# First forget gates computed from x before its norm, and the second half's recurrent steps placed at other slots

## The reference

```python
def rms_norm(x, g):
    y = x * rsqrt(mean(x * x, axis=-1) + RMS_EPS)
    return y * g

def trunk_layer(x, ...):
    h = rms_norm(x, g_mix_pre)
    proj = h @ w_in                      # q, f, i, g of the recurrence, q, k, v of attention
    f = lb + (1 - lb) * sigmoid(z_f)     # forget gate
    k = (1 - lb) * sigmoid(-z_f)
    o, state = gated_linear_recurrence(q, k, v, log(f), s0, chunk)
    rec = rms_norm(o, g_rec_out) * silu(z_g)          # the norm over each head
    mixed = concat([rec, attn]) @ w_out
    x = x + rms_norm(mixed, g_mix_post)
    h = rms_norm(x, g_mlp_pre)
    u = square(relu(h @ w_up))
    return x + rms_norm(u @ w_down, g_mlp_post)
```

## Time and profile before

| | us |
|---|---|
| median of 3 timed runs | 1590.98 (1590.57 to 1594.33) |
| the profiled execution, whole | 1592.15 |
| its span, first to last instruction | 1590.4 |
| mean granted TensorE clock, share of full | 0.993 |
| PE busy | 1536.7 |
| DVE busy | 997.5 |
| ACT busy | 850.3 |

### The profile page before, as it was taken

One profiled execution on the slowest core, in us unless ns is written; L12 is line 12 of the kernel. 1 busy time (PEld: TensorE's weight loads), 2 busy tenths in 40 slices (PEclk: granted clock), 3 DMA queues, 4 the chain that ended last, 5 costly groups with the idle time before them and its releaser, 6 DMA issues.

```text
span 1590.4 us, 29827 instructions
## 1 busy us (share of the span) xinstructions
PE 1536.7 (97%) x11984; PEld 1463.5 (92%) x11984; DVE 997.5 (63%) x1675; ACT 850.3 (53%) x1540; POOL 129.9 (8%) x165
## 2 busy tenths in 40 slices
PE   5999999899999999999999999998999999999996
PEld 5998789898999999999999987898899999999996
DVE  6683778774548655345887656878645675553466
ACT  6445655476455755234664565445755465551552
POOL 4120123000000000000002100330000000000000
PEclk9999999999999999999999999999999999999998
DMA  6644664353454555334443467343534545552453
GB/s 202 202 137 164 235 217 133 107 179 107 134 165 153 167 190 180 114 107 150 155 146 120 141 219 266 121 141 115 169 104 148 164 154 179 182 183 80 133 154 118
DMA packets 83237, 247.89 MB, mean 156 GB/s; under 512 B 8691, under 2 KB 26483, under 8 KB 82972
## 3 DMA queue, kind: packets, MB, share of 16 engines
q1 hardware_dynamic: 83100, 245.98, 48.2%
HBM read 234.13 MB, written 14.44 MB: 156 GB/s over the span
## 4 chain that ended last, share of the span: by engine, by line
PE 86%; DVE 8%; ACT 2%; issue 2%; DMA 1%; SPq 0%; DVEq 0%; ACTq 0%
PE ps L1030 68%; PE ps L1027 7%; PE ps L1083 3%; DVE w_rest L1347 2%; PE ps L1233 1%; PE ps L1220 1%; PE ps L1248 1%; DVE reg L1385 1%; DMA kc<-kcT 1%; DVE x L1389 1%; DVE norm_every L1370 1%; DVE square_sum L1360 1%; ACT w_high L749 1%; PE ps L1058 1%; PE ps L1206 0%
## 5 line engine op out<-in xcount | busy, mean ns | idle before, releaser
L1030 PE MATMUL ps<-h_high,w_rest 128*128 128x320 f32 (+1 forms) x1920 | 581.2, 303 | 8.5 <-DVE h_rest L1409 5.8
L1030 PE MATMUL ps<-h_rest,w_high 128*128 128x320 f32 (+1 forms) x1920 | 570.5, 297 | 0.0
L1030 PE MATMUL ps<-h_high,w_high 128*128 128x320 f32 (+1 forms) x1920 | 570.2, 297 | 0.0
L749 ACT ACTIVATE w_high<-w_raw 128x1024 fp32r<-128x1024 f32 x384 | 402.1, 1051 | 231.4 <-PE ps L1030 231.4
L1347 DVE TENSOR_TENSOR w_rest<-w_raw,w_high 128x1024 fp32r<-128x1024 f32 x380 | 473.0, 1250 | 74.7 <-ACT w_high L749 74.6
L1030 PEld LDWEIGHTS ps<-h_high,w_rest 128*128 128x128 f32 x1920 | 366.4, 191 | 26.1 <-issue 21.6
L1030 PEld LDWEIGHTS ps<-h_rest,w_high 128*128 128x128 f32 x1920 | 366.6, 191 | 0.8 <-issue 0.4
L1030 PEld LDWEIGHTS ps<-h_high,w_high 128*128 128x128 f32 x1920 | 366.5, 191 | 0.0
L1030 PE MATMUL ps<-u_high,w_rest 128*128 128x320 f32 (+1 forms) x1024 | 306.0, 299 | 2.8 <-DVE u_rest L1451 2.4
L1030 PE MATMUL ps<-u_high,w_high 128*128 128x320 f32 (+1 forms) x1024 | 303.8, 297 | 0.0
L1030 PE MATMUL ps<-u_rest,w_high 128*128 128x320 f32 (+1 forms) x1024 | 303.7, 297 | 0.0
(11 more groups left out here) (181 smaller groups left out, 1600.0 us busy)
## 6 DMA issues: line engine op xcount, KB each, us to landing
w_raw<-w SPq DMA_DIRECT2D x384, 512.0 KB, 3.6
kc<-kcT SPq DMA_DIRECT2D x16, 512.0 KB, 8.7
vc<-vc SPq DMA_DIRECT2D x16, 512.0 KB, 7.1
s_in<-s SPq DMA_DIRECT2D x8, 512.0 KB, 5.9
ss<-s_in SPq DMA_DIRECT2D x8, 512.0 KB, 5.9
bias<-rel_scratch SPq DMA_DIRECT2D x8, 512.0 KB, 4.5
rel_scratch<-rel_row SPq DMA_DIRECT2D x1, 2560.0 KB, 12.3
bias<-rel_scratch SPq DMA_DIRECT2D x8, 256.0 KB, 5.4
```

Of the source, the lines that this page charges most:

```text
L749: A.activation(whi[:, v % RING], raw[:, v % RING], ACT.Copy).then_inc(S["w_hi"], 1)
L1030: last = pe.matmul(ps[:, bank, 0:n], wt[:, slot, c, :], xt[:, c, :], **flags)
```

## The change

Two things, in one diff.

First products. ACT rounds `x * gain` (not yet normed) to `first_high`, DVE makes `first_rest`, and F0 to F3 of layer 0, half 0, multiply these. F0 and F1 are followed on PE by the norm's sum. Their results are multiplied by the inverse norm on DVE (`f_scaled`, into `tmp`) before ACT takes the two sigmoids from there. The six first products have six PSUM banks (`FIRST_BANKS`) instead of two. The first weight block is loaded ahead of x, the parameters behind x's first part, and DVE makes the remainder of block 0. ACT now rounds blocks 2 and 3 ahead of the norm's root, and blocks 4 and 5 (`N_SOON`) between the chunks of `pre`; DVE makes the remainders of blocks 4 and 5 within `pre` as well, ahead of the gates' arithmetic.

Second half's steps, in both layers: `upd` goes from behind IB 18 to behind IB 25, `out` from IB 23 to IB 27, `r_sum` from IB 25 to D0A 0, `r_spr` from IB 27 and U0A 0 to D0A 1 and D0A 2.

```diff
+FIRST_BANKS = (0, 1, 3, 4, 2, 7)
+N_FIRST = 4
+N_SOON = 2
...
-    put("IB", 18, "upd", 1)
+    put("IB", 25, "upd", 1)
...
-    put("IB", 23, "out", 1)
+    put("IB", 27, "out", 1)
...
-    put("IB", 25, "r_sum", 1)
-    put("IB", 27, "r_spr", 1, 0)
-    put("U0A", 0, "r_spr", 1, 1)
+    put("D0A", 0, "r_sum", 1)
+    put("D0A", 1, "r_spr", 1, 0)
+    put("D0A", 2, "r_spr", 1, 1)
...
         if o.i == 1:
+            here.insert(0, ("first_sum", 0))
             here.append(("rel", 0))
...
+            load(0)
             for c in range(0, KC, 2):
                 sp.dma_start(x[:, c:c + 2, 0:WIDE[0]], xT[:, c:c + 2, 0:WIDE[0]]).then_inc(S[f"x_part{c // 2}"], 16)
-            sp.dma_start(prm[:], par).then_inc(S["p_in"], 16)
-            for v in range(RING):
+                if c == 0:
+                    sp.dma_start(prm[:], par).then_inc(S["p_in"], 16)
+            for v in range(1, RING):
                 load(v)
...
                 if o.kind == "F":
+                    if o.n < N_FIRST:
+                        act.wait_ge(S["f_mul"], o.n + 1)
+                        src = tmp[:, o.n, 0:n]
                     A.activation(kb[o.h][:, o.k, :], src, ACT.Sigmoid, scale=-1.0)
...
             act.wait_ge(S["one_set"], 2)
+            act.wait_ge(S["p_in"], 16)
+            x_high(0)
+            high(0)
+            for p in range(1, 4):
+                x_high(p)
+            high(1)
             for p in range(4):
                 x_sq(0, 0, p)
-            high(0)
-            norm_sum(0, 0, 0)
-            high(1)
-            for p in range(4):
-                pre(0, 0, 0, p)
             high(2)
             high(3)
+            norm_sum(0, 0, 0)
             act.wait_ge(S["lb_set"], 2)
             A.activation(lb[:], lb[:], ACT.Exp).then_inc(S["lb_exp"], 1)
+            for p in range(4):
+                if p < N_SOON:
+                    act.wait_ge(S["blk"], p + 1)
+                    high(RING + p)
+                pre(0, 0, 0, p)
...
+            def f_scaled(o):
+                dve.wait_ge(S["blk"], o.n + 1)
+                V.tensor_tensor(tmp[:, o.n, 0:WIDE[0]], ps[:, bank_of(o), 0:WIDE[0]], every[:, 0:WIDE[0]], ALU.mult)\
+                    .then_inc(S["f_mul"], 1)
...
+            def x_low(c):
+                dve.wait_ge(S["x_hi"], c + 1)
+                V.scalar_tensor_tensor(first_l[:, c, :], x[:, c, 0:WIDE[0]], prm[:, 0, c:c + 1], first_h[:, c, :].bitcast(F32),
+                                       ALU.mult, ALU.subtract).then_inc(S["x_lo"], 1)
+
+            x_low(0)
+            x_low(1)
+            dve.wait_ge(S["w_hi"], 1)
+            V.tensor_tensor(wlo[:, 0], raw[:, 0], whi[:, 0].bitcast(F32), ALU.subtract).then_inc(S["w_lo_0"], 1)
+            for c in range(2, KC):
+                x_low(c)
             for p in range(4):
                 x_sq(0, 0, p)
-            norm_sum(0, 0, 0)
-            for p in range(5):
-                pre(0, 0, 0, p)
...
+            norm_sum(0, 0, 0)
+            dve.wait_ge(S["n_inv"], 1)
+            for o in outs[:2]:
+                f_scaled(o)
+            for p in range(5):
+                pre(0, 0, 0, p)
+                if p in (1, 4):
+                    rest(RING + p // 4)
```

More of the change, by code:

```diff
@@ L424, in build @@
             [place(f"bias1_{s}", [P, 2, 512], offset=o) for s, o in enumerate((o_vt[0], o_f))]]
+    first_h = place("first_high", [P, KC, WIDE[0]], F32R, offset=part(0, 8))
+    first_l = place("first_rest", [P, KC, WIDE[0]], F32R, offset=part(1, 0))
+    first_x = place("first_x", [P, KC, WIDE[0]], offset=part(1, 10))
     rel_sb = place("rel_sb", [P, NREL], offset=o_key[1])
@@ L448, in build @@
     free_at = {}
-    lo_of = {v: ("w_lo_p", v + 1) for v in range(RING)}
+    lo_of = {v: ("w_lo_p", v) if v else ("w_lo_0", 1) for v in range(RING)}
     for o in outs:
@@ L731, in a_spr @@
                                 ALU.subtract).then_inc(S["a_lo"], 1)
-            rest(0)
+            for v in range(1, RING):
+                rest(v)
             for c in range(1, KC, 2):
                 pool.wait_ge(S["h_hi"], c + 1)
-                V.tensor_tensor(hl[0][:, c, :], acc[0][:, c, :], hh[0][:, c, :].bitcast(F32), ALU.subtract).then_inc(S["h_odd"], 1)
-            for v in range(1, RING):
-                rest(v)
+                V.tensor_tensor(hl[0][:, c, :], first_x[:, c, :], hh[0][:, c, :].bitcast(F32), ALU.subtract).then_inc(S["h_odd"], 1)
             table = {"lev": lev, "wide": wide, "s_upd": s_upd, "kc_own": kc_own, "r_spr": r_spr, "a_spr": a_spr}
@@ L759, in x_sq @@
             def x_sq(l, h, p):
-                if h == 0:
-                    act.wait_ge(S[f"x_part{p}"], 16)
-                elif p == 0:
+                if h and p == 0:
                     act.wait_ge(S["x_in1"], 16)
@@ L1329, in a_spr, with first_sum @@
                     held[5 + i] = (S["a_scaled"], 8 * l + 4 * h + 2 * g + i + 1)
-            pe.wait_ge(S["one_set"], 2)
-            norm_sum(0, 0, 0)
-            table = {"norm_sum": norm_sum, "rel": rel, "lev": lev, "k_t": k_t, "v_t": v_t, "upd": upd, "out": out,
+            def first_sum(l):
+                pe.wait_ge(S["one_set"], 2)
+                norm_sum(0, 0, 0)
+            table = {"first_sum": first_sum, "norm_sum": norm_sum, "rel": rel, "lev": lev, "k_t": k_t, "v_t": v_t, "upd": upd, "out": out,
                      "s_rd": s_rd, "s_o": s_o, "s_upd": s_upd, "r_sum": r_sum, "r_spr": r_spr, "sc": sc_, "pt": pt_, "pv": pv,
@@ L1395, in pre @@
                 cols = slice(FIRST[h], FIRST[h] + n)
+                to = acc[h] if m else first_x
                 if p == 0:
                     dve.wait_ge(S["n_inv"], m + 1)
-                    if m == 0:
-                        dve.wait_ge(S["p_in"], 16)
                 if p < 4:
                     for c in (2 * p, 2 * p + 1):
-                        V.scalar_tensor_tensor(acc[h][:, c, :], x[:, c, cols], gain[:, c:c + 1], every[:, 0:n],
+                        V.scalar_tensor_tensor(to[:, c, :], x[:, c, cols], gain[:, c:c + 1], every[:, 0:n],
                                                ALU.mult, ALU.mult).then_inc(S["nap"], 1)
@@ L1416, in evict @@
                 n = WIDE[o.h]
[L1417 removed]
+                src = ps[:, bank_of(o), 0:n]
                 if o.kind in ("Q", "G"):
@@ L1730, in _ @@
                     rest(v)
-                late = [v + RING for v in free_at[o.n] if v + RING < n_loads]
+                late = [v + RING for v in free_at[o.n] if N_SOON <= v < n_loads - RING]
                 after(o)
```

39 lines of the change are left out of this document (27 added, 12 removed).

## The result

The changed kernel took **1598.43 us** (median of 5 runs, 1597.14 to 1600.17), the kernel before, timed beside it, 1591.7 (5 runs, 1590.57 to 1594.33). The ratio is 1.0039, 95% interval 1.0028 to 1.0049, so slower, by 4.5 to 7.8 us. The forecast was 1598.0. The profiled execution took 1600.17, with a span of 1598.4, 8.0 more than before.

What follows compares the result with a forecast made beforehand. PE, busy 97% of the span, was taken as the bound, so only its waits count. First products 4.3 plus second half's steps 2.8 gave 7.1 us slower, 1598.0 for the median; range 1587 to 1602, slower at chance 0.51.

Steps and rivals of the forecast that it cites:

- the sum of 7.1: Whole kernel: 4.3 us slower from the first products plus 2.8 slower from the second half's steps.
- Start of F0: First products: F0 starts at 11.2, 6.3 us earlier than before, with parameters taken to land at 6.8.
- Rival (d): Start: parameters still land at 8.2, F0 starts hardly earlier, time 1600; inside the forecast, given no separate chance.
- The root's end S: First products: the norm's root ends at 24.1 against 12.8 before; without POOL's hold about 22.8.
- From S to block 6: DVE and ACT work behind the root: block 6's remainder, which Q2 needs, ends at S+22.7 = 46.8.
- PE's wait and the clock: Ahead of Q2: PE waits 6.5 us from 40.3, half clock costs 2.0; behind Q3 PE is 4.3 later.
- The lower bound: First products: without holds S = 22.3, chain 2.0 shorter, block 6 at 43.0, hidden; at best 1.4 us faster.
- the upper bound: First products: parameters late (S = 25.5) and clock loss 2.4, 6.1 us slower; range stated up to +6.5.
- The second half's steps: Per layer: IB 22 sum 1.6 earlier, PE's wait 4.5, net 0.2 slower, new `pt` wait 1.25; 2.8 us for both layers.
- (a): First products: DVE catches up better, holds and handovers cost half, block 6 at 44 to 45; 1594, chance 0.24.
- (b): Behind IB 22: `upd` on DVE held the sum, PE's wait shrinks 1.6 per layer; 1592, chance 0.11.
- (c): At Q2: block 6's remainder ends by 40.3, PE keeps its 4.2 us lead; 1586.8 or 1585, chance 0.14.

Runs made afterwards that it cites:

- p1_nohold: `p1_only` with block 1's remainder made by DVE instead of POOL: 1594.01 us against 1592.3 for the kernel before, ratio 1.0007.
- p1_soon4: `p1_only` with `N_SOON = 4`, so blocks 6 and 7 are rounded and remaindered early too: 1596.18 us against 1592.83 for the kernel before.
- p1_defer: `p1_soon4` with F2 and F3 scaled ahead of the remainders, F0 to F3 arithmetic and second-half squares deferred: 1587.93 us against 1592.3 for the kernel before.
- p2_norm: The kernel before with only `r_sum` and `r_spr` moved to D0A 0, 1 and 2: 1594.48 us against 1592.3 for the kernel before.
- p2_only: The kernel before with only the second half's steps moved as in the change: 1593.66 us against 1592.83, ratio 1.0010.
- p2_fill: The kernel before with the second half's `upd` moved behind IB 22, ahead of the norm's sum: 1586.95 us against 1592.3, ratio 0.9965.
- p1_only: The changed kernel with the second half's steps back at their old slots: 1595.72 us against 1592.83 for the kernel before, ratio 1.0020.
- after_fill: The changed kernel with `upd` behind IB 22 and `out` back at IB 23: 1590.96 us against 1592.44 for the kernel before, ratio 0.9991.
- best: The kernel before with `p1_defer`'s first products, block 1's remainder on DVE and `upd` behind IB 22: 1580.45 us against 1592.44, ratio 0.9928.

## Why the prediction was right

**The time.** 1598.43 against 1598.0; the sum of 7.1 stands against 8.0 in the traces and 6.2 by the ratio (0.0039 times 1592), 4.5 to 7.8 by its interval. That the time agrees within 0.4 us is partly luck. The terms miss in both directions: the sum had 2.0 for the lower clock, where PE is 4.3 longer busy, and 5.1 of idle time, where 3.7 were added. The mechanism is what the rows below bear out.

**Start of F0.** 10.27, forecast 11.2. The parameters were there at 5.70 instead of the 6.8 that I took between 5.5 and 8.2. Rival (d), parameters late, is out.

**The root's end S.** 22.65, forecast 24.1. 1.1 of the difference is the parameters. That POOL's remainder holds the adds was right, and `p1_nohold` shows it: 1.07 us of S, where I had put 1.3 by the difference of the two estimates (24.1 and 22.8).

**From S to block 6.** Forecast S + 22.7; the remainder ends at 44.16 + 1.22, S + 22.7. It is right at its marks too: block 5's remainder ends at S + 13.2 (forecast 12.8), the scaling of F2 at S + 18.0, as forecast. What makes it long is what stands in the queue, which `p1_soon4` and `p1_defer` separate: the block alone sooner only moves the wait, with the arithmetic behind it the wait is gone. That is the shown cause of the first part's loss.

**PE's wait and the clock.** The wait is 4.6, forecast 6.5, as S came 1.45 sooner and Q1 ended about 0.5 later. The forecast had Q0 end 6.0 behind F3, for a product of 3.5, so it left room for waits there, and there are two for `h_rest`, 1.9 together. What it left out are the 3.4 us at half clock behind them, about 1.5 lost; F0's earlier start, 0.9, paid part of it. Behind the wait the loss was mis-sized the other way: from Q2 at 45.42, two products of 7.04 in all would give 52.46, and G0 came at 55.17, so 2.7 lost for the 2.0 I had charged. Together G0 is 3.67 late, forecast 4.3. The lower bound, block 6 at 43.0 and "hidden", was read wrongly: PE stands from 40.3, so 2.7 us of wait and the clock behind it belonged into it; and the upper bound comes to 6.1 by its terms, not 6.5.

**The second half's steps.** All three statements hold. The sum behind IB 22 moved 1.7 forward (forecast 1.6), PE's wait stayed (4.34, forecast 4.5), and the new wait at `pt` is 1.15 to 1.2 in each layer (forecast 1.25). Net 0.94 in layer 1, where the half-clock stretch is as long as before, and 2.09 in layer 0, where it is 6.8 us instead of 3.4: 3.0 in the sum, forecast 2.8. The size per layer was off in both directions, in layer 0 by the clock, for which the forecast had no term here; that the sum fits is luck in part. `p2_norm` shows that the norm's place alone brings the wait at `pt`, and its time alone (1.0012) is no less than that of `p2_only` (1.0010), so the rest of the part is too small for these runs to see.

**Rivals.** (a), DVE catching up by half, is out at S + 22.7. (b), that `upd` ahead of the inverse sets PE's wait behind IB 22, is out in the form I gave it, since PE arrives earlier by as much. `p2_fill` shows what was wrong with the place, not with the idea: taken away ahead of the inverse, `upd` let PE and DVE come forward alike, and the wait stayed 4.34; put between the inverse and the wait, it costs DVE's line nothing and shortens the wait by 1.8. (c), Q2 in time, needed a remainder at 40.3. In `p1_defer` it is there before 38.3, and that kernel takes 1587.93, where I had worked out 1586.8 with nothing lost in the second half.

**Left open.** Where and for how long PE falls to half clock differs between traces of kernels that are alike at that place: the stretch near 780 is in before and in `p1_nohold`, not in `p1_only`. Each is worth up to 1.5 us, and so the difference of two kernels in their spans carries that much, or more where several differ, beside the edit. I can't say which pattern of waits decides it.

## What to carry to other kernels

An earlier first product is worth nothing by itself: follow the line from the root to the last thing that an early product needs (here a weight block's remainder on VectorE), and put behind it whatever is read only later. Where TensorE must wait for a fixed time of another engine, move its own independent work into the wait, ahead of the waiting instruction; here 1.8 us of matmuls made the wait 1.8 us shorter each time, and behind five of six such waits (two each in `p2_fill`, `after_fill` and `best`) the clock stayed full as well. Before moving a step to a quieter stretch, look at what its PSUM banks and its results are next needed for there.

## What the runs showed of the hardware that I had not expected

A wait cut from 4.33 to 2.54 us left no half clock behind it in either layer of `p2_fill`, where 4.33 had left 3.4 and 6.8 us of it, but 3.4 us in layer 1 of `best`; and two waits within Q0 (1.4 and 1.1 us from matmul to matmul) were followed by 3.4 us at half clock in the changed kernel, and by none in `after_fill`, whose start is the same. So a wait's price here was its length plus 0 to 2.7 us. The example in the Trainium skill (TensorE: Matmul & The Clock Gate, on how HAM oscillation bites in real kernels) has 1.67 us at half clock behind each wait, 0.8 lost; the stretches in these traces are longer, 3.4 to 6.8.
